# Router weights over 256 tokens: scattered with an adding DMA into a table in DRAM instead of built by one-hot products

## The chip, the cores and the metric

The kernel runs on one core of one Trainium2 chip. The metric is the device time of one execution in microseconds (us). TensorE (PE in the profile), VectorE (DVE), ScalarE (ACT) and GpSimd (POOL) compute, SyncE (SP) issues most DMAs; GpSimd issues the indexed ones.

## The reference

Two transformer blocks in a row on 512 tokens of width 1024: the first with gated delta rule and sparse attention, the second with two recurrent mixers and, last, a layer that picks 128 of 16384 small experts for each token. The change is in that last layer, which computes:

```python
s_top, i_top = lax.top_k(s, 16)                       # per head (8) and half (2), 128 keys each
cand = s_top[:, :, 0, :, None] + s_top[:, :, 1, None, :]
cand_idx = i_top[:, :, 0, :, None] * 128 + i_top[:, :, 1, None, :]
best, pos = lax.top_k(cand.reshape(n, 8, 256), 16)
idx = jnp.take_along_axis(cand_idx.reshape(n, 8, -1), pos, axis=-1)
w = jax.nn.softmax(best, axis=-1)
act = jax.nn.gelu(jnp.einsum('nhkd,nd->nhk', jnp.take(u_tab, idx, axis=0), hb))
out = jnp.einsum('nhk,nhkd->nd', w * act, jnp.take(v_tab, idx, axis=0))
```

## The kernel before, in words

The last layer is computed densely for 448 of the 512 tokens: for all 16384 experts the kernel takes the gelu of u times h, multiplies it by a table of weights W[expert, token] that is zero where the token did not choose the expert, and multiplies by v. The other 64 tokens gather their rows of u and v from DRAM by index.

*The u stage* (`u_pe`, `u_sc`, `u_ve`, `u_sy`) goes over 128 tiles of 128 experts. TensorE multiplies each fp32 product as three products of a high and a low half (`hh`, `hl` by `wh`, `wl`), 24 matmuls of 448 columns for a tile. ScalarE makes the high half `wh` of a weight pair, VectorE the low half `wl`, once for two tiles. ScalarE writes the gelu to `gst`, one of two buffers, and SP spills it to `gelu_spill`.

*The choice* runs woven into the u stage by a generator, `together(..., CHOOSE)`: CHOOSE steps of `choose` for each step of u. `top(j)` finds the experts of 128 tokens (j is 0 to 3) on VectorE and ends with the weights in `sel[:, 2]` (semaphore `wsel`). `hot(j)` builds the table for them, in quads of four tokens: VectorE makes one-hot matrices `Bh` and weighted one-hots `Ah`, TensorE multiplies them into 128 x 128 tables, ScalarE copies these to `stage`, SP spills 64 tokens at a time to `weight_spill`. 112 quads cover the 448 tokens.

*The v stage* goes over 64 pairs of tiles. `fetch` on SP brings back gelus and weights (`gv`, `wv`), `weigh` on VectorE multiplies them, `upper` and `lower` split the product in two halves `ph` and `pl`, and TensorE multiplies by v. The first three fetches, and the first `weigh` and `lower`, stand in the queues of SP and VectorE before the last tiles of the u stage (`start` at the end of `choose`). They wait until the whole table is in DRAM. All that stands behind them in the same queue waits too: on SP the loads of u and the gelu spills, on VectorE the low halves of u.

GpSimd does next to nothing before the v stage: one small DMA, then 128 gathers of 128 rows each (`gather_po`).

Of the kernel before, what the change touches and what calls it, by code (L numbers as in the profile page):

```python
# [22 lines left out]
class Line:  # L23
# [17 lines left out]
    def settle(self):  # L41
# [30 lines left out]
    [("g2_ex", 1), ("g3_ex", 1), ("sga", 16)],  # L72
    [("ve", 1356), ("fin", 8)],
# [97 lines left out]
ND = 512 - GT  # L171
# [100 lines left out]
def _build(nc, D, ctx):  # L272
# [90 lines left out]
    with ExitStack() as ar:  # L363
        x1 = sb("x1", [128, 8, 512], F32, ar)
        nb[1] = norm_bufs(1, ar)
        nb[2] = nb[1]
        ffh = sb("ffh", [128, 11, 512], R32, ar)
        ffl = sb("ffl", [128, 11, 512], R32, ar)
        fcv = [sb(f"fcv{j}", [128, 512], F32, ar) for j in range(6)]

    with ExitStack() as ar:
# [78 lines left out]
    with ExitStack() as ar:  # L450
        s_ = sb("s_", [128, 16, 128], F32, ar)
        sr = sb("sr", [128, 256], F32, ar)
        top = sb("top", [128, 16, 16], F32, ar)
        tix = sb("tix", [128, 16, 16], U32, ar)
        best = sb("best", [128, 8, 16], F32, ar)
        pix = sb("pix", [128, 8, 16], U32, ar)
        pa = sb("pa", [128, 8, 16], U32, ar)
        paf = sb("paf", [128, 2, 128], F32, ar)
        sel = sb("sel", [128, 3, 128], F32, ar)
        ijw = sb("ijw", [128, 3, 128], F32, ar)  # L460
        red8 = sb("red8", [128, 2, 8], F32, ar)
        tops = [top, cols[:, 0:256].rearrange("p (n k) -> p n k", n=16), top, top]
        tixs = [tix, cst[:, 256:512].bitcast(U32).rearrange("p (n k) -> p n k", n=16), tix, tix]
        Ah = [sb(f"Ah{j}", [128, 4, 128], F32, ar) for j in range(3)]
        Bh = [sb(f"Bh{j}", [128, 4, 128], F32, ar) for j in range(3)]
        stage = [sb(f"stage{j}", [128, 128, 64], F32, ar) for j in range(2)]
        gst = [sb(f"gst{j}", [128, ND], F32, ar) for j in range(2)]
    cand = eq = s_[:, :, :].rearrange("p (h x) k -> p h (x k)", h=8)

    with ExitStack() as ar:  # L470
        gv = [sb(f"gv{j}", [128, 2, ND], F32, ar) for j in range(3)]
        wv = [sb(f"wv{j}", [128, 7, 2, 64], F32, ar) for j in range(3)]
# [12 lines left out]
        nb[4] = norm_bufs(4, ar)  # L485
# [1225 lines left out]
    def ffn_ve(v):  # L1711
# [10 lines left out]
        for half in range(2):  # L1722
# [19 lines left out]
            for n in range(8):  # L1742
# [1149 lines left out]
    def top_ve(v, j):  # L2892
# [11 lines left out]
        v.settle()  # L2904
        for h in range(8):
            v.then_inc(tt(cand[:, h, :].rearrange("p (a b) -> p a b", a=16), bc(top[:, 2 * h, :], 16),
                          rep(top[:, 2 * h + 1, :], 16), A_), s("ve"))
        v.settle()
# [11 lines left out]
        for c in range(2):  # L2920
            v.settle()
            for h in range(8):
                e3 = eq[:, h, :].rearrange("p (k a) -> p k a", k=16)
                v.then_inc(tt(e3, bc(paf[:, c, 16 * h:16 * h + 16], 16), rep(C["iota"][:, 0:16], 16), ALU.is_equal),
                           s("ve"))
            yield
            v.settle()
            for h in range(8):
                e3 = eq[:, h, :].rearrange("p (k a) -> p k a", k=16)
                v.then_inc(tt(e3, e3, rep(top[:, 2 * h + c, :], 16), M), s("ve"))  # L2930
            yield
            if j and c == 0:
                v.wait_ge(s("ijw_mm"), j)
            v.settle()
# [9 lines left out]
        v.settle()  # L2944
        v.then_inc(tt(w3, w3, bc(red8[:, 1, :], 16), M), s("wsel"))
        if j == 0:
# [12 lines left out]


    def quads(j):

        return [(32 * j + q - 16, q) for q in range(16 if j == 0 else 0, 32)]

    WST = 256, 192

    def hot_pe(p, j):
# [3 lines left out]
        if j:  # L2971
            p.wait_ge(s("ijw"), j)
        for c in range(3):
# [5 lines left out]
        for t, q in quads(j):  # L2979
# [3 lines left out]
            for z in range(4):  # L2983
                ins = mm(p, bank[5 + t % 3][:, 128 * z:128 * z + 128], [(Ah[t % 3][:, z, :], Bh[t % 3][:, z, :])],
                         start=z == 0, check=False)
# [20 lines left out]
    def hot_ve(v, j):  # L3006
        for _ in range(3):
            yield
        v.wait_ge(s("ijw_mm"), j + 1)
        if j:  # L3010
            v.wait_ge(s("ab"), 32 * j - 16)
        v.then_inc(v.e.tensor_copy(flat(ijw[:, :, :]), bank[4][:, 0:384]), s("ijw"))
        v.settle()
        for t, q in quads(j):
            if t >= 3:
                v.wait_ge(s("ab_mm"), t - 2)
            v.e.tensor_tensor(Bh[t % 3][:, :, :], rep(C["iota"], 4), bc(ijw[:, 1, 4 * q:4 * q + 4], 128), ALU.is_equal)
            for z in range(4):
                k = 4 * q + z
                ins = v.e.tensor_scalar(Ah[t % 3][:, z, :], C["iota"], ijw[:, 0, k:k + 1], ijw[:, 2, k:k + 1],  # L3020
                                        ALU.is_equal, M)
            v.then_inc(ins, s("ab"))
            yield
        for _ in range(3):
            yield
# [76 lines left out]

    CHOOSE = 1.06

# [7 lines left out]
    def experts_ve(v):  # L3112
        arrive(v, 9)
        next_low(v, "u", 0)
        together((u_ve(v), 1), (choose_ve(v), CHOOSE))

# [18 lines left out]

    def weigh(v, i):
        v.wait_ge(s(f"gv{i % 3}"), 32 * (i // 3 + 1))
        g4 = gv[i % 3][:, :, :].rearrange("p x (b t) -> p x b t", b=7)
        for x in range(2):
            ins = v.e.tensor_tensor(g4[:, x], g4[:, x], wv[i % 3][:, :, x, :], M)  # L3140
        v.then_inc(ins, s("gw"))

# [74 lines left out]
    def start_pe(p):  # L3217
        p.wait_ge(s("ijw"), 4)
        turned_pe(p, 0)
# [30 lines left out]
    def v_pe(p):  # L3250
        p.wait_ge(s("stg"), 112)
        p.wait_ge(s("hT"), 2)
# [205 lines left out]
    def pool(e):  # L3458
        g = Line(e)
        gprep_po(g)  # L3460
        gather_po(g)

# [119 lines left out]
```

## Time and profile before

| | |
|---|---|
| median of 3 runs | 3344.34 us (3343.17 to 3346.76) |
| profiled execution, its own time | 3348.95 us |
| its span from first to last instruction | 3347.1 us |
| TensorE busy | 3244.8 us, 97% of the span |
| VectorE, ScalarE, GpSimd busy | 2110.6, 1188.1, 177.3 us |
| mean granted TensorE clock | 0.975 of 2.4 GHz |

A busy engine is one whose queue has an instruction under way. Times in rows are microseconds from the start of the span. The u stage lies at about 1975 to 2708 us, the v stage from there to 3327 us.

### The profile page before, as it was taken

Reading aid. Unit: us, or ns where it says so; the run is one execution under the profiler, and the core shown is the slowest. Engines: PE = TensorE matmul, PEld = TensorE weight load, DVE = VectorE, ACT = ScalarE, POOL = GpSimd, SP = SyncE. Lnnn points to the kernel's source line nnn. Section 1 sums busy time; section 2 is a strip of 40 time slices with the busy share of each in tenths; the row PEclk is TensorE's granted clock in tenths of the full one; section 3 lists DMA queues with packets and bytes.
Section 4 is the critical chain, followed back from the end, with each engine's and each line's share of the span. In section 5 each row is a group of like instructions: output and inputs, shape, how many; then the busy total and the mean of one; then the engine's idle time right before and its main releaser. Section 6 shows DMA issues by size and latency. Waiting matters only on the chain.

```text
span 3347.1 us, 43205 instructions
## 1 busy us (share of the span) xinstructions
PE 3244.8 (97%) x17902; PEld 2899.0 (87%) x17902; DVE 2110.6 (63%) x3746; ACT 1188.1 (35%) x1585; POOL 177.3 (5%) x137
## 2 busy tenths in 40 slices
PE   7998999999999999999999999999999999999998
PEld 7887887878789889888778788999999999999998
DVE  6446865747534434667544589796977356767775
ACT  2244233222223423555532223444445332222222
POOL 0000000000000000000000000000000013233230
PEclk9888999999999998999999999999999999999999
DMA  5232113232231242112233333545456678898884
GB/s 229 96 113 114 52 39 113 79 116 81 101 115 60 76 161 84 64 64 89 87 121 145 115 129 130 205 165 205 150 183 224 211 250 316 322 319 316 321 313 155
DMA packets 213763, 520.82 MB, mean 156 GB/s; under 512 B 12320, under 2 KB 143904, under 8 KB 178112
## 3 DMA queue, kind: packets, MB, share of 16 engines
q1 hardware_dynamic: 192944, 442.92, 36.8%
q0 software_dynamic: 18464, 67.15, 6.0%
q10 hardware_dynamic: 2160, 7.99, 0.6%
q8 instruction: 142, 2.33, 0.3%
q14 instruction: 53, 0.43, 0.0%
HBM read 437.23 MB, written 80.74 MB: 155 GB/s over the span
## 4 chain that ended last, share of the span: by engine, by line
PE 86%; DVE 7%; ACT 4%; issue 1%; DMA 1%; SPq 0%; DVEq 0%; ACTq 0%
PE bank L570 79%; PE bank L1233 2%; PE bank L634 1%; DVE wl L525 1%; PE bank L2504 1%; ACT wh L518 1%; PE bank L582 1%; PE bank L641 1%; ACT sgm L2572 1%; PE bank L1498 0%; PE bank L2513 0%; DVE ub L3186 0%; DMA cst<-in_consts 0%; DVE acc L148 0%; ACT sgm L2576 0%
## 5 line engine op out<-in xcount | busy, mean ns | idle before, releaser
L570 PE MATMUL bank<-hh,wh 128*128 128x512 f32 (+2 forms) x2512 | 949.5, 378 | 15.0 <-DVE hl L148 5.4
L570 PE MATMUL bank<-hl,wh 128*128 128x512 f32 (+2 forms) x2512 | 921.0, 367 | 0.0
L570 PE MATMUL bank<-hh,wl 128*128 128x512 f32 (+2 forms) x2512 | 920.0, 366 | 0.0
L525 DVE TENSOR_TENSOR wl<-ring,wh 128x2048 fp32r<-128x2048 f32 (+2 forms) x249 | 554.5, 2227 | 554.0 <-ACT wh L518 553.3
L518 ACT ACTIVATE wh<-ring 128x2048 fp32r<-128x2048 f32 (+2 forms) x249 | 463.4, 1861 | 879.2 <-PE bank L570 870.7
L570 PEld LDWEIGHTS bank<-hh,wh 128*128 128x128 f32 x2512 | 481.8, 192 | 83.7 <-issue 18.4
L570 PEld LDWEIGHTS bank<-hl,wh 128*128 128x128 f32 x2512 | 481.2, 192 | 64.1 <-issue 6.3
L570 PEld LDWEIGHTS bank<-hh,wl 128*128 128x128 f32 x2512 | 480.2, 191 | 61.8
L570 PE MATMUL bank<-ph,wh 128*128 128x448 f32 x1024 | 372.4, 364 | 5.3 <-DVE pl L3151 5.3
L570 PE MATMUL bank<-ph,wl 128*128 128x448 f32 x1024 | 370.7, 362 | 0.0
L570 PE MATMUL bank<-pl,wh 128*128 128x448 f32 x1024 | 369.9, 361 | 0.0
L570 PEld LDWEIGHTS bank<-ph,wh 128*128 128x128 f32 x1024 | 192.1, 188 | 19.9 <-issue 8.1
L570 PEld LDWEIGHTS bank<-ph,wl 128*128 128x128 f32 x1024 | 192.0, 188 | 13.6
L570 PEld LDWEIGHTS bank<-pl,wh 128*128 128x128 f32 x1024 | 191.9, 187 | 12.8
L3001 ACT ACTIVATE stage<-bank 128x512 f32<-128x512 f32 x112 | 123.7, 1108 | 94.7 <-PE bank L570 94.7
L570 PE MATMUL bank<-wh,hh 128*128 128x256 f32 (+2 forms) x520 | 156.2, 300 | 0.0
L570 PE MATMUL bank<-wl,hh 128*128 128x256 f32 (+2 forms) x520 | 151.1, 291 | 0.0
L570 PE MATMUL bank<-wh,hl 128*128 128x256 f32 (+2 forms) x520 | 151.0, 290 | 0.0
L3174 POOL DMA_INDIRECT ub<-in_urow,gsel x64 | 84.3, 1318 | 858.7 <-DMA weight_spill<-stage 537.1
L3020 DVE TENSOR_SCALAR Ah<-cst,ijw 128x128 f32<-128x128 f32 x448 | 124.5, 342 | 0.0
L570 PEld LDWEIGHTS bank<-Bh,Ah 128*128 128x128 f32 x896 | 116.9, 191 | 3.2 <-issue 0.4
L570 PE MATMUL bank<-Bh,Ah 128*128 128x128 f32 x896 | 117.7, 275 | 0.0
(516 smaller groups left out, 4348.6 us busy)
## 6 DMA issues: line engine op xcount, KB each, us to landing
ring<-in_v SPq DMA_DIRECT2D x68, 1024.0 KB
ring<-in_u SPq DMA_DIRECT2D x64, 1024.0 KB
gelu_spill<-gst SPq DMA_DIRECT2D x128, 224.0 KB, 1.9
weight_spill<-stage SPq DMA_DIRECT2D x28, 1024.0 KB, 8.6
gv<-gelu_spill SPq DMA_DIRECT2D x64, 448.0 KB, 4.6
wv<-weight_spill SPq DMA_DIRECT2D x64, 448.0 KB, 7.3
ring<-in_ada SPq DMA_DIRECT2D x24, 1024.0 KB
ring<-in_wup SPq DMA_DIRECT2D x22, 1024.0 KB
```

The costliest lines, as they stand in the source:

```text
L518: a.then_inc(a.e.activation(wh[q % 2][:, 0:n], ring[k % 4][:, 0:n], ACT.Copy), s("whi"))
L525: v.then_inc(v.e.tensor_tensor(wl[q % 2][:, 0:n], ring[k % 4][:, 0:n], wh[q % 2][:, 0:n].bitcast(F32), S_), s("parts"))
L570: ins = p.e.matmul(out, l, r, start=start and i == 0, stop=stop and i == len(pairs) - 1, skip_group_check=not check)
L582: return p.e.transpose(out, in_, ident[0:k, 0:k])
L634: ins = p.e.matmul(out[:, j:j + 1], sq[:, 128 * j:128 * j + 128], C["ones"][:, 0:1], start=start and j == 0, stop=stop, skip_group_check=True)
L641: ins = p.e.matmul(out[:, 128 * j:128 * j + 128], r[:, j:j + 1].to_broadcast([128, 128]), ident, start=j == 0, stop=True, skip_group_check ...
L1233: ins = p.e.matmul(ps[:, 128 * h:128 * h + 128], l, r, start=h == 0 and n_ == 0, stop=True, skip_group_check=True)
L2504: p.then_inc(p.e.matmul(bank[7][:, :], l, r, start=True, stop=True), s("ss_mm"))
L2572: ins = a.e.activation(sg[:, h, :], bank[3 + h // 4][:, 128 * (h % 4):128 * (h % 4) + 128], ACT.Abs, bias=nac[:, j, 8 * g + h:8 * g + h + 1])
L3001: a.then_inc(a.e.activation(place[:, :, 4 * (q % 16):4 * (q % 16) + 4].rearrange("p j t -> p t j"), quad(bank[5 + t % 3][:, :]), ACT.Copy) ...
L3020: ins = v.e.tensor_scalar(Ah[t % 3][:, z, :], C["iota"], ijw[:, 0, k:k + 1], ijw[:, 2, k:k + 1], ALU.is_equal, M)
L3174: g.e.indirect_dma_start(ub[n % 4][:, :], None, D["urow" if n < 64 else "vrow"], bass.IndirectOffsetOnAxis(gsel[:, 0, n % 64:n % 64 + 1], ...
```

## The change

The table for the 256 tokens of j = 1 and j = 2 is no longer built by `hot`. It is a second table in DRAM, `weight_scatter` (64 pairs x 2 x 128 x 256 values, 16.8 MB).

- It is cleared by 16 DMAs of 1 MB from a zeroed tile, issued from GpSimd during the first block's feed-forward part (`cleared_po`).
- VectorE computes for each chosen expert the flat place in the table (`sidx`) and leaves the weights in `swt`, one buffer for each of the two j (`top_ve`).
- GpSimd issues 2 x 128 indexed DMAs (`scatter_po`). Each writes 128 single values, one for each partition (token), to 128 places, adding to what is there. One DMA holds one of the 16 choices of one head. The 16 of a head follow each other freely; before the next head GpSimd waits until all earlier ones have landed, since two heads of one token may name the same expert.
- `hot` stays for j = 0 (16 quads) and j = 3 (32 quads), with two `Ah`/`Bh` buffers instead of three. 64 quads are gone.
- The first fetches wait for all 256 scatters (`scat`), a fetch is five DMAs instead of two, a `weigh` one instruction instead of two.
- In `top_ve` eight instructions on 256 elements become one on 2048, at five places. CHOOSE goes from 1.06 to 0.8.

```diff
+    SCATTER, HOT = (1, 2), (0, 3)
     def quads(j):
-        return [(32 * j + q - 16, q) for q in range(16 if j == 0 else 0, 32)]
+        return [(q - 16, q) for q in range(16, 32)] if j == 0 else [(16 + q, q) for q in range(32)]
...
+    def cleared_po(g):
+        arrive(g, 3)
+        g.then_inc(g.e.memset(zeros[:, :], 0.0), s("zr"))
+        g.wait_ge(s("zr"), 1)
+        flat_w = sw_.rearrange("i x b t -> (i x b t)").rearrange("(p n f) -> p n f", p=128, f=2048)
+        for n in range(16):
+            g.e.dma_start(flat_w[:, n, :], zeros[:, :]).then_inc(s("zw").sem, 16)
+
+    def scatter_po(g):
+        cells = sw_.rearrange("i x b t -> (i x b t)").unsqueeze(1)
+        g.wait_ge(s("zw"), 256)
+        for x, j in enumerate(SCATTER):
+            g.wait_ge(s("wsel"), j + 1)
+            g.wait_ge(s("scr"), x + 1)
+            for h in range(8):
+                if h:
+                    g.wait_ge(s("scat"), 16 * (128 * x + 16 * h))
+                for k in range(16 * h, 16 * h + 16):
+                    g.e.indirect_dma_start(cells, bass.IndirectOffsetOnAxis(sidx[x][:, k:k + 1], 0), swt[x][:, k:k + 1],
+                                           None, compute_op=ALU.add).then_inc(s("scat").sem, 16)
...
-        for j in range(3):
-            yield from weave((hot(j), 1), (top(j + 1), 0.75))
+        yield from weave((hot(0), 1), (top(1), 0.75))
+        yield from top(2)
+        yield from top(3)
         yield from hot(3)
         yield from start
...
-    CHOOSE = 1.06
+    CHOOSE = 0.8
...
         if i < 3:
-            y.wait_ge(s("ab_mm"), 112)
+            y.wait_ge(s("ab_mm"), 48)
+            y.wait_ge(s("scat"), 4096)
...
-        y.e.dma_start(wv[i % 3][:, :, :, :].rearrange("p b x t -> p b (x t)"),
-                      wd_[:, i].rearrange("b i x t -> i b (x t)")).then_inc(s(f"gv{i % 3}").sem, 16)
+        w = wv[i % 3]
+        y.e.dma_start(w[:, :, 64:320], sw_[i].rearrange("x b t -> b x t")).then_inc(s(f"gv{i % 3}").sem, 16)
+        for b, c in enumerate((0, 320, 384)):
+            y.e.dma_start(w[:, :, c:c + 64], wd_[b, i]).then_inc(s(f"gv{i % 3}").sem, 16)
...
     def pool(e):
         g = Line(e)
+        cleared_po(g)
         gprep_po(g)
+        scatter_po(g)
         gather_po(g)
```

GpSimd's queue from the second block on, before the change (`kdm` belongs to the recurrent mixer, `ub` are the gathers):

```order
L1957 TENSOR_TENSOR kdm<-kdm,km 128x16 [waits u_sr] x4
L3168 DMA gsel<-gsel 64x2x64 [waits gsel]
L3174 DMA ub<-in_urow,gsel 128x1024 [waits wst1,gcr]
L3174 DMA ub<-in_urow,gsel 128x1024 x3
L3174 DMA ub<-in_urow,gsel 128x1024 [waits gd] x60
```

The same stretch after the change; the pair of rows in its middle, 1 and 15 scatters, stands there 16 times in all:

```order
L1965 TENSOR_TENSOR kdm<-kdm,km 128x16 [waits u_sr] x4
L3008 DMA weight_scatter<-swt,sidx 4194304x1 [waits scr,h,zw]
L3008 DMA weight_scatter<-swt,sidx 4194304x1 x15
L3008 DMA weight_scatter<-swt,sidx 4194304x1 [waits scat]
...
L3214 DMA gsel<-gsel 64x2x64 [waits gsel]
L3220 DMA ub<-in_urow,gsel 128x1024 [waits wst1,gcr]
```

All 256 scatters stand ahead of GpSimd's first gather.

SP's queue at the first two fetches before the change, behind the 111th spill of a gelu tile (`in_u` are the loads of u):

```order
L3036 DMA weight_spill<-stage 128x16x128 [waits cvs]
L3036 DMA weight_spill<-stage 128x16x128 x3
L3100 DMA gelu_spill<-gst 128x448 [waits hi]
L3132 DMA gv<-gelu_spill 128x896 [waits gst1,wst0,wst1,gst0,cmp_h]
L3133 DMA wv<-weight_spill 128x7x128
L3132 DMA gv<-gelu_spill 128x896 [waits gst1,gst0]
L3133 DMA wv<-weight_spill 128x7x128
```

The same place after the change, now behind the 99th spill:

```order
L3145 DMA gelu_spill<-gst 128x448 [waits hi]
L3080 DMA weight_spill<-stage 128x16x128 [waits cvs]
L3080 DMA weight_spill<-stage 128x16x128 x3
L3179 DMA gv<-gelu_spill 128x896 [waits wst0,gst1,gst0,wst1,scat,cmp_h]
L3181 DMA wv<-weight_scatter 128x2x256
L3183 DMA wv<-weight_spill 128x2x64 x3
L3179 DMA gv<-gelu_spill 128x896 [waits gst1,gst0]
L3181 DMA wv<-weight_scatter 128x2x256
L3183 DMA wv<-weight_spill 128x2x64 x3
```

The fetch has moved 12 tiles of u forward, and waits for `scat` as well. On VectorE the end of `top(1)`, where the first scatters' weights come out, stands four low halves `wl` (eight tiles) later than before, and that of `top(2)` nine low halves behind it.

## Rows read from the trace of the kernel before

**Rows 1.** The page: busy shares, and the last chain by engine and line.

```profile
PE 3244.8 (97%) x17902; PEld 2899.0 (87%) x17902; DVE 2110.6 (63%) x3746; ACT 1188.1 (35%) x1585; POOL 177.3 (5%) x137
PE 86%; DVE 7%; ACT 4%; issue 1%; DMA 1%; SPq 0%; DVEq 0%; ACTq 0%
```

**Rows 2.** Stretches: length, busy time (count) by engine, clock, DMA share, GB/s.

```profile
540.00:640.00 100.00, 95.38 (x408) 77.17 (x407) 71.05 (x85) 29.41 (x33) 0.00 (x0) 0.95 0.23 81
...
2150.00:2250.00 100.00, 100.00 (x561) 94.01 (x560) 91.61 (x288) 43.06 (x43) 0.00 (x0) 1.00 0.46 159
...
2615.00:2650.00 35.00, 33.18 (x203) 29.81 (x202) 8.81 (x8) 7.93 (x10) 0.00 (x0) 0.97 0.98 296
...
2712.00:3327.00 615.00, 609.69 (x3054) 569.18 (x3053) 426.00 (x448) 172.18 (x130) 171.20 (x124) 1.00 0.85 303
```

**Rows 3.** TensorE's groups in 2150:2250.

```profile
L570 PE MATMUL bank<-hh,wh 128*128 128x448 f32 x139 | 52.1, 375 | 0.0
L570 PE MATMUL bank<-Bh,Ah 128*128 128x128 f32 x144 | 19.0, 275 | 0.0
```

**Rows 4.** The chain behind the table's last spill: start, length, what.

```profile
2614.10 1.02 ACT stage L3001
...
2625.64 8.93 DMA weight_spill<-stage
...
2634.69 0.33 SPq L3132
...
2636.15 7.07 DMA wv<-weight_spill
...
2645.40 2.22 DVE wl L525
...
2647.66 12.36 PE bank L570 x52
```

**Rows 5.** VectorE's timeline: the end of `top(1)`.

```profile
2142.72 0.29 DVE L2945 TENSOR_TENSOR sel<-sel,red 128x128 f32<-128x128 f32 x1
```

**Rows 6.** GpSimd's timeline: start, length, then in brackets its idle time before.

```profile
2043.09 0.81 POOL L3168 DMA_DIRECT2D gsel<-gsel  x1 [904.67 <-DVE gsel L2949]
2581.05 1.01 POOL L3174 DMA_INDIRECT ub<-in_urow,gsel  x1 [537.14 <-DMA weight_spill<-stage]
2582.36 0.95 POOL L3174 DMA_INDIRECT ub<-in_urow,gsel  x1 [0.30 <-issue]
2583.62 0.94 POOL L3174 DMA_INDIRECT ub<-in_urow,gsel  x1 [0.30 <-issue]
...
2996.88 1.85 POOL L3174 DMA_INDIRECT ub<-in_vrow,gsel  x1 [0.31 <-issue]
...
3014.79 1.93 POOL L3174 DMA_INDIRECT ub<-in_vrow,gsel  x1 [7.38 <-DVE acc L148]
3017.03 0.94 POOL L3174 DMA_INDIRECT ub<-in_vrow,gsel  x1 [0.30 <-issue]
```

**Rows 7.** VectorE's timeline beside those gathers.

```profile
2582.42 1.11 DVE L3020 TENSOR_SCALAR Ah<-cst,ijw 128x128 f32<-128x128 f32 x4
...
2996.84 1.09 DVE L3151 TENSOR_TENSOR pl<-gv,ph 128x896 fp32r<-128x896 f32 x1
...
3013.24 2.67 DVE L148 SCALAR_TENSOR_TENSOR acc<-ub,gwt,acc 128x1024 f32<-128x1024 f32 x2
```

**Rows 8.** VectorE's groups over the u stage, 1975:2712.

```profile
L525 DVE TENSOR_TENSOR wl<-ring,wh 128x2048 fp32r<-128x2048 f32 x64 | 146.4, 2288 | 145.1 <-ACT wh L518 144.8
L3020 DVE TENSOR_SCALAR Ah<-cst,ijw 128x128 f32<-128x128 f32 x448 | 124.5, 342 | 0.0
L3017 DVE TENSOR_TENSOR Bh<-cst,ijw 128x512 f32<-128x512 f32 x112 | 76.4, 682 | 11.5 <-PE bank L570 11.3
```

**Rows 9.** Landing time of the tile `gsel`, the one plain DMA from GpSimd.

```profile
DMA to landing us min/median/max: 2.6/2.6/2.6
```

**Rows 10.** DMA issues: count, size, median us to landing.

```profile
gelu_spill<-gst SPq DMA_DIRECT2D x128, 224.0 KB, 1.9
weight_spill<-stage SPq DMA_DIRECT2D x28, 1024.0 KB, 8.6
```

**Rows 11.** What SP's queue waited for in 1975:3340: us, times, longest.

```profile
SPq L3132 <- DVE pl L3151: 489.1, 60, 9.5
```

More of the change, by code:

```diff
@@ L463, in _build @@
         tixs = [tix, cst[:, 256:512].bitcast(U32).rearrange("p (n k) -> p n k", n=16), tix, tix]
-        Ah = [sb(f"Ah{j}", [128, 4, 128], F32, ar) for j in range(3)]
-        Bh = [sb(f"Bh{j}", [128, 4, 128], F32, ar) for j in range(3)]
+        Ah = [sb(f"Ah{j}", [128, 4, 128], F32, ar) for j in range(2)]
+        Bh = [sb(f"Bh{j}", [128, 4, 128], F32, ar) for j in range(2)]
+        sidx = [sb(f"sidx{j}", [128, 128], U32, ar) for j in range(2)]
+        swt = [sb(f"swt{j}", [128, 128], F32, ar) for j in range(2)]
+        sdiag = sb("sdiag", [128, 128], F32, ar)
+        stok = sb("stok", [128, 16], F32, ar)
+        sb("past_scatter", [128, 368], F32, ar)
         stage = [sb(f"stage{j}", [128, 128, 64], F32, ar) for j in range(2)]
@@ L471, in _build @@
         gv = [sb(f"gv{j}", [128, 2, ND], F32, ar) for j in range(3)]
-        wv = [sb(f"wv{j}", [128, 7, 2, 64], F32, ar) for j in range(3)]
+        wv = [sb(f"wv{j}", [128, 2, ND], F32, ar) for j in range(3)]
         sb("past_choice", [128, 1936], F32, ar)
@@ L2904, in top_ve @@
         v.settle()
-        for h in range(8):
-            v.then_inc(tt(cand[:, h, :].rearrange("p (a b) -> p a b", a=16), bc(top[:, 2 * h, :], 16),
-                          rep(top[:, 2 * h + 1, :], 16), A_), s("ve"))
+        pairs = top[:, :, :].rearrange("p (h c) k -> p h c k", c=2)
+        v.then_inc(tt(cand[:, :, :].rearrange("p h (a b) -> p h a b", a=16),
+                      pairs[:, :, 0, :].unsqueeze(3).to_broadcast([128, 8, 16, 16]),
+                      pairs[:, :, 1, :].unsqueeze(2).to_broadcast([128, 8, 16, 16]), A_), s("ve"))
         v.settle()
@@ L2921, in top_ve @@
             v.settle()
[L2922 to L2925, printed above, removed]
+            places = eq[:, :, :].rearrange("p h (k a) -> p (h k) a", a=16)
+            v.then_inc(tt(places, bc(paf[:, c, :], 16), rep(C["iota"][:, 0:16], 128), ALU.is_equal), s("ve"))
             yield
             v.settle()
-            for h in range(8):
-                e3 = eq[:, h, :].rearrange("p (k a) -> p k a", k=16)
-                v.then_inc(tt(e3, e3, rep(top[:, 2 * h + c, :], 16), M), s("ve"))
+            e4 = eq[:, :, :].rearrange("p h (k a) -> p h k a", k=16)
+            v.then_inc(tt(e4, e4, pairs[:, :, c, :].unsqueeze(2).to_broadcast([128, 8, 16, 16]), M), s("ve"))
             yield
-            if j and c == 0:
-                v.wait_ge(s("ijw_mm"), j)
+            if j == 1 and c == 0:
+                v.wait_ge(s("ijw_mm"), 1)
             v.settle()
@@ L2944, in top_ve @@
         v.settle()
-        v.then_inc(tt(w3, w3, bc(red8[:, 1, :], 16), M), s("wsel"))
+        if j in SCATTER:
+            x = SCATTER.index(j)
+            v.then_inc(tt(swt[x][:, :].rearrange("p (h k) -> p h k", h=8), w3, bc(red8[:, 1, :], 16), M), s("wsel"))
+            v.then_inc(stt(v.e, sel[:, 0, :], sel[:, 1, :], 128.0, sel[:, 0, :], M, A_), s("ve"))
+            v.settle()
+            v.then_inc(ts(v.e, sidx[x][:, :], sel[:, 0, :], 256.0, M, stok[:, x:x + 1], A_), s("scr"))
+        else:
+            v.then_inc(tt(w3, w3, bc(red8[:, 1, :], 16), M), s("wsel"))
         if j == 0:
@@ L3008, in hot_ve @@
             yield
-        v.wait_ge(s("ijw_mm"), j + 1)
+        v.wait_ge(s("ijw_mm"), HOT.index(j) + 1)
         if j:
-            v.wait_ge(s("ab"), 32 * j - 16)
+            v.wait_ge(s("ab"), 16)
         v.then_inc(v.e.tensor_copy(flat(ijw[:, :, :]), bank[4][:, 0:384]), s("ijw"))
@@ L3014, in hot_ve @@
         for t, q in quads(j):
[L3015 to L3017 removed]
+            if t >= 2:
+                v.wait_ge(s("ab_mm"), t - 1)
+            v.e.tensor_tensor(Bh[t % 2][:, :, :], rep(C["iota"], 4), bc(ijw[:, 1, 4 * q:4 * q + 4], 128), ALU.is_equal)
             for z in range(4):
                 k = 4 * q + z
[L3020 removed]
+                ins = v.e.tensor_scalar(Ah[t % 2][:, z, :], C["iota"], ijw[:, 0, k:k + 1], ijw[:, 2, k:k + 1],
                                         ALU.is_equal, M)
@@ L3132, in fetch @@
         y.e.dma_start(gv[i % 3][:, :, :], gd_[i]).then_inc(s(f"gv{i % 3}").sem, 16)
-        y.e.dma_start(wv[i % 3][:, :, :, :].rearrange("p b x t -> p b (x t)"),
-                      wd_[:, i].rearrange("b i x t -> i b (x t)")).then_inc(s(f"gv{i % 3}").sem, 16)
+        w = wv[i % 3]
+        y.e.dma_start(w[:, :, 64:320], sw_[i].rearrange("x b t -> b x t")).then_inc(s(f"gv{i % 3}").sem, 16)
+        for b, c in enumerate((0, 320, 384)):
+            y.e.dma_start(w[:, :, c:c + 64], wd_[b, i]).then_inc(s(f"gv{i % 3}").sem, 16)
     def weigh(v, i):
[L3137 to L3141, printed above, removed]
+        v.wait_ge(s(f"gv{i % 3}"), 80 * (i // 3 + 1))
+        v.then_inc(v.e.tensor_tensor(gv[i % 3][:, :, :], gv[i % 3][:, :, :], wv[i % 3][:, :, :], M), s("gw"))
     def upper(a, i):
```

35 lines of the change are left out of this document (23 added, 12 removed).

## The prediction, on record before the run

> **What bounds the kernel now.** I read the busy shares first, then the stretches of the last layer, then the chain behind the table's last spill. TensorE is busy for 97% of the span and holds 86% of the chain that ended last [rows 1]. Inside the u stage it is busy for 100.00 of 100.00 us while VectorE is too at 91.61 [rows 2]: VectorE is nearly full there, but TensorE waits for nothing. So an instruction taken off TensorE there is time saved, if nothing else becomes late.
>
> The one tight place is where the table is finished. The last `stage` copy is at 2614.1; its spill lands at 2634.6; only then does SP issue the first fetch (2634.69), whose data land at 2643.2; VectorE, which has been standing in `weigh`, then makes the low half that is due, and TensorE starts on it at 2647.66 [rows 4]. TensorE lost 1.8 us of 35 there [rows 2]. The reader should see two things. The chain from the table's completion to TensorE is 13 us long, and TensorE has no reserve behind it: whatever makes the fetch later than "last `stage` copy plus 20.5 us" stops TensorE for as long.
>
> **What the change takes away.** 64 quads, each 4 one-hot products, each of 2 records: 512 of the `Bh,Ah` matmuls. In 2150:2250 TensorE ran 3 x 139 matmuls of 448 columns and 144 of these [rows 3]. One of 448 columns costs 0.2005 us: the v stage runs 64 x 48 = 3072 of them in 615 us [rows 2]. So 417 x 0.2005 = 83.6 us, and the other 16.4 us are 144 records: 0.114 us each. 512 x 0.114 = 58 us. **Term 1: -58 us.** The copies to `stage`, 16 of the 28 MB of spills, and 64 x (0.68 + 4 x 0.28) = 115 us of VectorE go too (0.28 is a quarter of the 1.11 us of four [rows 7]); they were hidden under TensorE and give nothing by themselves. The merged instructions in `top_ve` are hidden in the same way.
>
> **What it adds.** *Clearing.* 16 MB of stores during the first feed-forward part, where the DMA engines are at 0.23 and the load is 81 GB/s [rows 2]. At the v stage's 303 GB/s they take 55 us beside the loads, which run several tiles ahead: 0, and at most a few us if a weight comes late. *Fetch.* Five DMAs instead of two. In the v stage SP waits 489 us for VectorE's `pl` [rows 11], so 64 x 3 issues of about 0.43 us are covered: 0. For the first fetches nothing covers them: 2 x 3 x 0.43, **term 2: +3 us**.
>
> *The scatters.* They start when `top(1)` ends: 2143.0 before [rows 5], now 8 tiles later. A tile is 24 x 0.2005 = 4.81 us, so 2143 + 38.5 = 2182. `top(2)` ends 18 tiles, 87 us, behind that, sooner than 128 scatters can be issued, so GpSimd runs through. The fetch would be ready at 2634.6 less 12 tiles (57.7) less the 58 us of missing quads: 2519. GpSimd has 337 us for 256 scatters: 1.32 us for each, everything included, and 1.53 with term 1 spent.
>
> No row shows a scatter with single values or with an addition. The nearest is a gather of GpSimd: also 128 indexed rows in one DMA. Back to back it takes 0.94 us, with 0.30 us between two [rows 6], a period of 1.25: 256 x 1.25 = 320 us. Lower bound of one: the plain DMA from GpSimd, 0.81 + 0.30 = 1.11, 284 us. Upper bound: if an adding transfer must describe two reads where a copy describes one, the 0.94 doubles: 2.19, 561 us. I take 1.25, since count of rows and index are the same.
>
> *Restarts.* 15 times GpSimd waits for the last scatter to land. The plain DMA from GpSimd landed after 2.6 us [rows 9], a gelu spill after 1.9, a weight spill after 8.6 [rows 10]. With a landing after 4 us, between these, and 1.25 already counted, 15 x 2.75 = 41 us; with 2.6 us it is 20, with 8.6 it is 110.
>
> *VectorE holds GpSimd up.* A gather is not always 0.94 us. The one at 2996.88 started 0.04 us after `pl`, a TENSOR_TENSOR with both inputs in SBUF that ran 2996.84 to 2997.93, and ended at 2998.73, that is 0.80 us after it. The one at 3014.79 started inside two SCALAR_TENSOR_TENSOR that ended at 3015.91, and ended 0.81 us after them. The gather at 2582.36 lay beside four TENSOR_SCALAR and took its 0.95 [rows 6, 7]. So an instruction with two SBUF tensors makes a gather wait until it is over. In the v stage there were two or three gathers for each pair of tiles; now there is one each 1.25 us, so every `wl` of 2.29 us [rows 8] catches one. It waits for what is left, on average 2.29 - 1.25/2 = 1.67 us. 337 us hold 337/9.63 = 35 `wl`: 58 us. The merged instructions of 2048 elements have two SBUF inputs too, five in each of `top(2)` and `top(3)`, about 2.2 us each if they run at `wl`'s rate: 10 x 1.6 = 16 us. The 32 `Bh` of `hot(3)`, 0.68 us: 0.68/1.25 of them hit, for 0.34 us, 6 us. Together 80 us, bounds 0 and about 110 (each `Ah` held too).
>
> The Trainium skill, "SBUF — State Buffer", section "Who interferes with whom", says the same of VectorE instructions with two SBUF inputs beside a GpSimd instruction that reads SBUF, but also that a `tensor_tensor` was not seen to hold up descriptor generation. The row at 2996.88 shows one that did. By that last rule the sum would be the first rival below.
>
> 320 + 41 + 80 = 441 us, so the last scatter lands at 2182 + 441 = 2623, 104 us after the fetch could have gone. SP stands in the first fetch all that time. Behind it are the gelu spills: with two `gst` buffers ScalarE stops two tiles later, and with it `wh`; VectorE stops in `weigh`, and with it `wl`. TensorE follows at once, since rows 4's chain left it nothing. **Term 3: +104 us.** GpSimd's gathers begin behind the scatters but before the v stage, so nothing is late next.
>
> The sum is -58 + 3 + 104 = +49 us. The profiled execution took 3348.95, 4.6 above the median, and its span plus 1.85; the difference applies to both: 3344.3 + 49 = 3393 us at the median.
>
> **The rivals.**
> *The scatters fit (other side: faster).* If `wl` does not hold scatters up, because their index is read in a moment that mostly falls elsewhere, they take 361 us and end at 2543, 24 us late: -58 + 3 + 24 = -31, 3313 us. With the short restarts (20) they are 3 us late: 3292 us. For it speaks the gather beside four TENSOR_SCALAR, against it both long gathers of rows 6. It decides when a scatter costs less than 1.53 us with everything: from there down the kernel is faster. Chance 0.32.
> *The addition costs more.* 32768 single values are each read, added and written. If that costs the 0.94 again, 240 us more: 3393 + 240 = 3633 us; half of it, 3513. For it: an add reads two things; against: no row has one. Chance 0.24. The Trainium skill, "Collectives: The Full Stack", section "The bandwidth ceiling: the fold count and why AG ≠ RS ≠ AR", says that a reducing transfer passes two read descriptors for each piece where a copy passes one, and ran at about half the rate. No row here shows it; by it this rival would hold in full.
> *It balances.* Between the two, gain and wait are equal, at 1.53 us for a scatter: 3344 us. Chance 0.04.
>
> **How the numbers follow.** The forecast, scatters at a gather's price with VectorE in the way, has 0.40; its own range is 3355 to 3450, from 40 us less blocking to 8.6 us landings. A measurement tells 0.2% (7 us) from no change. Faster: 0.32. Same: 0.04. Slower: 0.40 + 0.24 = 0.64. The range goes from 3294, which leaves out only scatters fully hidden (0.06), to 3560, between the half and the full price of the addition (0.12 above it).
>
> **What would show it.** Term 1: in the u stage 24 matmuls a tile and no gap of their own, the last `stage` copy near 2498. Term 3: GpSimd's scatters from about 2182 to about 2623, most of 0.94 us, some near 2.5 that end 0.8 us behind a `wl`; SP waiting for a scatter for about 100 us; TensorE idle for as long around 2530 to 2630. Term 2: the first `weigh` some 11 us after the last landing. I am wrong if GpSimd is done before 2519 (faster by the full 58), if scatters back to back take much more than 0.94 with VectorE idle, which shows in the last ones, when VectorE stands still, or if the DMA engines and not GpSimd set the pace, seen in waits for `scat` much longer than 3 us.

## The result, and the profile after

| | before | after |
|---|---|---|
| median | 3344.34 us (5 runs, 3338.11 to 3350.36) | 3512.65 us (5 runs, 3511.1 to 3518.81) |
| profiled execution, span | 3347.1 us | 3509.3 us |
| mean granted TensorE clock | 0.975 | 0.947 |

The change costs 168 us: 1.0509 times the time before (95% interval 1.0496 to 1.0521). The forecast was 3393 us, +49, in a range of 3294 to 3560. Direction, place and chain were as forecast; the size was not.

The page of after: span, busy shares, the granted clock in 40 slices, the packets of GpSimd's DMAs, the last chain by engine, and two of the costliest groups.

```profile
span 3509.3 us, 41968 instructions
PE 3185.0 (91%) x17384; PEld 2838.7 (81%) x17384; DVE 1994.0 (57%) x3227; ACT 1119.3 (32%) x1521; POOL 628.2 (18%) x410
...
PEclk9889999999999989999999999999955799999999
...
q0 software_dynamic: 57632, 84.08, 9.5%
...
PE 72%; POOL 12%; DVE 6%; issue 4%; ACT 4%; DMA 2%; SPq 0%; DVEq 0%; ACTq 0%; POOLq 0%
...
L577 PE MATMUL bank<-hh,wh 128*128 128x512 f32 (+2 forms) x2512 | 945.3, 376 | 237.2 <-ACT gst L3128 213.9
...
L3008 POOL DMA_INDIRECT weight_scatter<-swt,sidx x256 | 440.9, 1722 | 1160.0 <-DVE sidx L144 1046.6
```

Beside [rows 1], TensorE is busy for 59.8 us less (3244.8 to 3185.0, 518 recorded matmuls fewer): the 58 us of the missing quads are there. GpSimd now holds 12% of the chain, and TensorE has one idle time of 213.9 us. The average of 91% says little: all of it is in one place.

Four stretches of after (length, busy time and count of PE, PEld, DVE, ACT, POOL, clock, DMA share, GB/s): the scatters beside the u stage, the stop, the clearing, the v stage.

```profile
2181.00:2515.00 334.00, 320.96 (x1708) 296.75 (x1707) 245.48 (x613) 125.52 (x127) 265.46 (x144) 0.99 0.62 164
2540.00:2680.00 140.00, 1.87 (x10) 1.39 (x8) 0.00 (x0) 0.00 (x0) 109.01 (x71) 0.52 0.20 0
540.00:640.00 100.00, 95.21 (x414) 77.08 (x414) 72.43 (x86) 30.24 (x36) 0.00 (x0) 0.97 0.46 180
2862.00:3477.00 615.00, 610.25 (x3048) 569.63 (x3046) 424.21 (x385) 176.03 (x134) 170.77 (x124) 1.00 0.88 306
```

The last two answer to [rows 2] (95.38 and 609.69 us of TensorE there): clearing the table is free although the DMA share doubles to 0.46, and a fetch of five DMAs costs the v stage nothing. In 2540:2680 only GpSimd works.

The scatters as a group (duration min/median/max in ns, first and last start), and what GpSimd's idle time before them ended with (us, times).

```profile
L3008 POOL DMA_INDIRECT weight_scatter<-swt,sidx x256: 1548/1550/3879, 2182.8 to 2735.5; - x128
...
  issue: 84.0, 241
  DMA weight_scatter<-swt,sidx: 29.3, 14
```

A scatter takes 1.55 us, and as the minimum is 1.548, never less. The 0.94 us of a gather [rows 6] was the forecast. The last lands at 2738.4, not 2623. The group of the 100 scatters that start in 2542:2738, when VectorE stands still, has the same mean, so it is not VectorE that makes them long:

```profile
L3008 POOL DMA_INDIRECT weight_scatter<-swt,sidx x100 | 155.1, 1551 | 41.5 <-issue 31.5 <-DMA weight_scatter<-swt,sidx 10.0
```

The waits of after: what the engines, and in the last row SP's queue, waited for in 1975:2900 (us, times, longest).

```profile
ACT gst L3128 <- DMA gelu_spill<-gst: 234.9, 5, 225.9
DVE gv L3187 <- DMA wv<-weight_spill: 219.5, 2, 214.7
PE bank L577 <- ACT gst L3128: 213.9, 1, 213.9
...
PE bank L577 <- DVE wl L532: 13.0, 9, 2.5
...
SPq L33 <- DMA weight_scatter<-swt,sidx: 212.9, 1, 212.9
```

SP stands 212.9 us in front of the first fetch, with all inputs but the scatters there; ScalarE, VectorE and TensorE stand behind it, each by about as much. TensorE stops 16 us after SP does (it works until 2541.9) and starts again 17 us after SP, so its stop is as long as the fetch is late. The critical chain of after at the end of the stop (start, length, what):

```profile
2735.49 2.91 DMA weight_scatter<-swt,sidx
2738.40 0.02 SPq L33
...
2750.55 4.65 DMA gelu_spill<-gst
...
2755.22 0.55 ACT gst L3128
...
2755.82 4.48 PE bank L577 x11
```

From the last scatter's landing (2738.40) to TensorE's start it is 17.4 us, 12 of them SP's issue of three fetches (15 DMAs) ahead of the gelu spill for which ScalarE waits. It was 13 us behind the last `weight_spill` [rows 4], and there `weigh` released TensorE, here the gelu spill. The stop has a small cost behind it as well: the first 14 matmuls follow each other at 0.37 us, with the granted clock at 0.54 in 2755:2762, and the next ones at 0.20 with 1.00, which is 2.4 us.

### The profile page after: what moved, and what is told of

It is laid out like the page before. It is cut to its first block, busy times and chain, and to the rows that moved or that the text cites. A ratio compares the mean times of both kernels' runs of the same rounds, so it can differ in the third digit from the quotient of the medians.

```text
span 3509.3 us, 41968 instructions
## 1 busy us (share of the span) xinstructions
PE 3185.0 (91%) x17384; PEld 2838.7 (81%) x17384; DVE 1994.0 (57%) x3227; ACT 1119.3 (32%) x1521; POOL 628.2 (18%) x410
## 4 chain that ended last, share of the span: by engine, by line
PE 72%; POOL 12%; DVE 6%; issue 4%; ACT 4%; DMA 2%; SPq 0%; DVEq 0%; ACTq 0%; POOLq 0%
PE bank L577 66%; POOL weight_scatter L3008 12%; PE bank L1240 2%; DMA weight_scatter<-swt,sidx 2%; PE bank L641 1%; PE bank L2512 1%; ACT wh L525 1%; DVE wl L532 1%; PE bank L648 1%; ACT sgm L2580 1%; PE bank L589 1%; PE bank L1505 0%; DMA cst<-in_consts 0%; PE bank L2521 0%; DVE ub L3232 0%
## 5 line engine op out<-in xcount | busy, mean ns | idle before, releaser
L577 PE MATMUL bank<-hh,wh 128*128 128x512 f32 (+2 forms) x2512 | 945.3, 376 | 237.2 <-ACT gst L3128 213.9
L525 ACT ACTIVATE wh<-ring 128x2048 fp32r<-128x2048 f32 (+2 forms) x249 | 463.3, 1861 | 930.4 <-PE bank L577 922.0
L3008 POOL DMA_INDIRECT weight_scatter<-swt,sidx x256 | 440.9, 1722 | 1160.0 <-DVE sidx L144 1046.6
L3187 DVE TENSOR_TENSOR gv<-gv,wv 128x896 f32<-128x896 f32 x64 | 69.4, 1084 | 219.5 <-DMA wv<-weight_spill 219.5
L3128 ACT ACTIVATE gst<-bank 128x448 f32<-128x448 f32 x128 | 68.3, 534 | 371.9 <-DMA gelu_spill<-gst 234.9
L3220 POOL DMA_INDIRECT ub<-in_vrow,gsel x64 | 90.2, 1410 | 202.0 <-DVE acc L148 179.6
```

The source lines that it names most:

```text
L525: a.then_inc(a.e.activation(wh[q % 2][:, 0:n], ring[k % 4][:, 0:n], ACT.Copy), s("whi"))
L577: ins = p.e.matmul(out, l, r, start=start and i == 0, stop=stop and i == len(pairs) - 1, skip_group_check=not check)
L3008: g.e.indirect_dma_start(cells, bass.IndirectOffsetOnAxis(sidx[x][:, k:k + 1], 0), swt[x][:, k:k + 1], None, compute_op=ALU.add).then_inc( ...
L3128: a.then_inc(a.e.activation(gst[t % 2][:, :], bank[t % 4][:, 0:ND], ACT.Gelu_apprx_tanh), s("ge_u"))
L3187: v.then_inc(v.e.tensor_tensor(gv[i % 3][:, :, :], gv[i % 3][:, :, :], wv[i % 3][:, :, :], M), s("gw"))
L3220: g.e.indirect_dma_start(ub[n % 4][:, :], None, D["urow" if n < 64 else "vrow"], bass.IndirectOffsetOnAxis(gsel[:, 0, n % 64:n % 64 + 1], ...
```

## The experiments

Times are medians, and a ratio is to runs of the kernel before that stand beside them. The edits show the lines that matter; sizes, buffer counts and semaphore numbers that follow from them are left out. Two theories were put against each other first: the addition makes a scatter long (A), or the 128 single values or indices do (B); and whether the scatters are the only loss.

**1. Scatters without the addition** (two heads that name one expert for a token then overwrite each other: the sums are left out).

```diff
 g.e.indirect_dma_start(cells, bass.IndirectOffsetOnAxis(sidx[x][:, k:k + 1], 0), swt[x][:, k:k + 1],
-                       None, compute_op=ALU.add).then_inc(s("scat").sem, 16)
+                       None).then_inc(s("scat").sem, 16)
```

> The 256 scatters write without adding (where two heads of a token name the same expert, the last one stays: this leaves out the addition). Theory A, the addition makes a scatter dearer than a gather: back to back it falls from 1.55 to about 0.94 us, the scatters take some 156 us less, TensorE's stop of 214 us falls to about 60, time about 3357 us. Theory B, single values written to DRAM cost it and not the addition: 1.55 us stays and the time stays within 5 us of 3513.

3379.47 us, ratio 1.009 [1.007, 1.011]. Its page has the packets of GpSimd's DMAs:

```profile
q0 software_dynamic: 28960, 84.08, 7.4%
```

The group of its scatters (ns min/median/max):

```profile
L3008 POOL DMA_INDIRECT weight_scatter<-swt,sidx x256: 962/967/3532, 2184.6 to 2605.4; - x128
```

Its waits, TensorE's and SP's:

```profile
PE bank L577 <- ACT gst L3128: 48.3, 1, 48.3
...
PE bank L577 <- issue: 19.1, 22, 2.5
...
SPq L33 <- DMA weight_scatter<-swt,sidx: 74.8, 1, 74.8
```

Theory A: 0.967 us, a gather's price within 0.03, in place of 1.550. The addition costs 0.58 us for each DMA, and without it the median goes from 3512.65 to 3379.47, 133 us less. It shows in the packets too: 28672 fewer, 112 for each of the 256 DMAs. The run took about 20 us more than expected; TensorE stood 19.1 us with nothing in the profile that it waited for ("issue"), of which more under 6. The executions were 3372.48, 3377.91, 3381.03 and 3463.31 us; the last, at a mean granted clock of 0.949, isn't in the ratio and has no trace, so whether it had more of these waits is open.

**2. Only j = 1 scattered** (the weights of 128 tokens are left out).

```diff
-        for x, j in enumerate(SCATTER):
+        for x, j in enumerate(SCATTER[:1]):
...
-            y.wait_ge(s("scat"), 4096)
+            y.wait_ge(s("scat"), 2048)
```

> Only the scatters of j = 1 are issued and waited for; the weights of 128 tokens are left out of the table. Theory: the wait for the scatters is the whole loss, and all other parts of the change (clearing, five DMAs for a fetch, merged instructions, CHOOSE 0.8) cost nothing: the last scatter lands near 2182 + 278 = 2460, before the fetch can go at 2519, TensorE does not stop, and the time is 3344 - 58 + 3 = 3289 us. Rival: one of the other parts costs something too: then the time is above 3300 us by as much.

3300.87 us, ratio 0.9864 [0.9848, 0.9881]. The 128 scatters, 1.55 us each, lie between 2189.3 and 2480.0, before the fetch is ready. SP waits for none; TensorE waits for this:

```profile
PE bank L577 <- DVE wl L532: 14.2, 10, 2.5
```

So term 1 is real, and the loss is the scatters' length. The rival of the expectation has a small part in it: 43 us came, not 58. 9.3 of the missing 15 are a wait for `wl` that before doesn't have, which in after lies ahead of the stop and costs nothing there; most of the rest is that the traced execution of before lay 4.6 us above its median (the two spans differ by 46.8). That the wait comes since `top(2)` and `top(3)`, without quads between them, run too densely at CHOOSE 0.8, and VectorE makes a low half late, is what 5 tests.

**3. Scatters of 64 values** (half of the scattered weights are left out).

```diff
-  bass.IndirectOffsetOnAxis(sidx[x][:, k:k + 1], 0), swt[x][:, k:k + 1],
+  bass.IndirectOffsetOnAxis(sidx[x][0:64, k:k + 1], 0), swt[x][0:64, k:k + 1],
```

> Each of the 256 scatters has 64 rows instead of 128 (the weights of the other 64 tokens of each j are left out). If the price goes by the row, 1.55 falls to about 0.8 us, the scatters take some 190 us less and end near 2548, time about 3300 us. If it is mostly fixed for each DMA, 1.55 stays and the time stays within 15 us of 3513.

3480.74 us, ratio 1.0405 [1.0388, 1.0422]; TensorE stops for 181.2 us. That is 32 us under the 3513 of a fixed price and 181 above the 3300 of a price by the row. From its page GpSimd's packets, then the group of its scatters:

```profile
q0 software_dynamic: 41248, 84.01, 8.8%
```

```profile
L3008 POOL DMA_INDIRECT weight_scatter<-swt,sidx x256: 1389/1397/4147, 2184.0 to 2703.2; - x128
```

Half of the values take 0.15 us off 1.55: nine tenths of the price stay with the DMA. The packets, though, go with the values (64 fewer for 64 fewer values), so the packets are not what the time goes by.

**4. CHOOSE 0.65**: the steps of VectorE's second queue are spread over more tiles; nothing is left out.

```diff
-    CHOOSE = 0.8
+    CHOOSE = 0.65
```

> CHOOSE 0.65 instead of 0.8, nothing left out: the scatters start about 9 tiles (43 us) later, and the first fetch moves from tile 99 to about tile 122. Theory: the scatters keep their 556 us and end near 2781, but nearly all of the u stage is done by then, so the v stage can start some 20 us after that, near 2800 instead of 2862: time about 3450 us, still slower than 3344. Rival: if the scatters were slowed by the work beside them and not by their own price, they end earlier and the time falls further, towards 3400.

3456.39 us, ratio 1.0328 [1.0311, 1.0346]. The scatters run from 2225.8 to 2786.3, 8 us longer than in after, but the table's other half is finished later too, and u tiles are made meanwhile. SP waits 162.4 us, TensorE 3.1 for `wl`, and the stop has moved to the v stage:

```profile
PE bank L577 <- DVE pl L3197: 173.9, 2, 173.6
```

**5. Both, 2 and 4** (the weights of 128 tokens are left out).

```diff
-        for x, j in enumerate(SCATTER):
+        for x, j in enumerate(SCATTER[:1]):
...
-            y.wait_ge(s("scat"), 4096)
+            y.wait_ge(s("scat"), 2048)
...
-    CHOOSE = 0.8
+    CHOOSE = 0.65
```

> As the run with the scatters of j = 1 alone (the weights of 128 tokens are left out), with CHOOSE 0.65. That run was 43 us faster than before instead of 58; TensorE waited 13 us for low halves wl in 2185:2370, where top(2) and top(3) run without a hot beside them. Theory: VectorE had more work there for each pair of tiles than TensorE; spread thinner the wait falls to about 3 us, time about 3291 us. Rival: the 13 us come from GpSimd holding VectorE up at the shared port, or from something else that CHOOSE does not touch: then 3301 stays.

3294.58 us, ratio 0.9855 [0.984, 0.987]. The wait for `wl` falls from 14.2 to 3.5 us, beside the same 128 scatters, so it isn't they that make `wl` late; waits for `pl` of 7.2 us come (6.2 in one). That is 6 us by the medians, but the intervals of the ratios overlap: the wait for `wl` moved as the theory says, but its worth is not measured.

**6. 64 values and no addition** (leaves out what 1 and 3 do).

```diff
-  bass.IndirectOffsetOnAxis(sidx[x][:, k:k + 1], 0), swt[x][:, k:k + 1],
-  None, compute_op=ALU.add)
+  bass.IndirectOffsetOnAxis(sidx[x][0:64, k:k + 1], 0), swt[x][0:64, k:k + 1],
+  None)
```

> 64 rows in each scatter and no addition (half of the weights left out). The adding scatter cost 1.55 us with 128 rows and 1.39 with 64, the plain one 0.97 with 128. If the addition is a fixed price for each DMA, the plain one with 64 rows costs 0.97 - 0.16 = 0.81; if part of it goes by the row, more, up to 0.97. Time about 3345 us, since the scatters end some 30 us earlier than in the run without the addition (3379).

3582.81 us, ratio 1.0715 [1.0698, 1.0731]: a clear miss, the slowest of all, with the shortest scatters. Their group, then TensorE's wait:

```profile
L3008 POOL DMA_INDIRECT weight_scatter<-swt,sidx x256: 886/892/2760, 2183.6 to 2579.9; - x128
```

```profile
PE bank L577 <- issue: 246.4, 137, 3.7
```

The stretches 2250:2350 and 2350:2450 of this kernel (busy PE, PEld, DVE, ACT, POOL, clock, DMA share, GB/s), and two rows of TensorE's timeline:

```profile
2250.00:2350.00 100.00, 19.16 (x36) 10.26 (x36) 13.38 (x46) 2.34 (x2) 71.43 (x79) 0.50 0.05 13
2350.00:2450.00 100.00, 80.83 (x351) 69.25 (x351) 62.12 (x151) 23.77 (x25) 24.25 (x26) 0.84 0.35 119
```

```profile
2484.71 0.53 PE L577 MATMUL bank<-hh,wh 128*128 128x448 f32 x1 [1.57 <-issue]
2487.51 0.53 PE L577 MATMUL bank<-hl,wh 128*128 128x448 f32 x1 [2.27 <-issue]
```

For pricing it still serves: 0.89 against 1.39 us, so the addition costs 0.50 at 64 values and 0.58 at 128. But while the scatters run, TensorE starts a matmul only every 2.80 us, at half clock (1.2 GHz), VectorE has 46 instructions in 100 us, and the DMA engines are at 0.05. TensorE waits for no engine and no transfer that the profile shows; ScalarE and VectorE also have waits that it puts down to a queue it doesn't know (208 and 59 us). The second stretch shows that the scatters are the cause: GpSimd, whose first 128 were done, stands there for 67 us before the next 128, and in 2362:2422 TensorE has 275 matmuls in 60 us at clock 0.93. Some 10 us after the scatters begin again it is slow again, and after the last ones the usual rate is back. Experiment 1 shows the same rows for a short time around 2530 to 2560 (matmuls of 0.53 us at clock 0.58, behind waits for "issue" of up to 1.9 us). How plain single-value scatters hold TensorE up, and why 64 values are worse than 128, is open.

**7. Scatter only what fits.** If 128 scatters are hidden and 256 are not, j = 1 alone should be scattered and 0, 2 and 3 built as before: 32 quads off, 32 x 8 x 0.114 = 29 us to gain. Nothing is left out, here and in 8 to 10.

```diff
-    SCATTER, HOT = (1, 2), (0, 3)
+    SCATTER, HOT = (1,), (0, 2, 3)
...
         yield from top(2)
-        yield from top(3)
+        yield from weave((hot(2), 1), (top(3), 0.75))
         yield from hot(3)
...
-    CHOOSE = 0.8
+    CHOOSE = 0.9
```

> Nothing left out: only j = 1 is scattered (128 scatters, with the addition), hot stays for j = 0, 2 and 3 (80 quads), top(3) woven with hot(2) again, CHOOSE 0.9. Theory: the scatters run from about 2170 to 2450 and are done long before the fetch at about 2600, so the saving is that of 32 quads, 32 x 0.91 = 29 us: 3315 us, up to 3320 if VectorE is late in the unwoven top(2). Rival: the scatters or the many small DMAs of a fetch (seven) cost something of their own: 3330 and above.

3332.07 us, ratio 0.9967 [0.9955, 0.9979]. No wait for scatters, but 16.9 us for `wl` in four waits (three of them, 12.3 us, where `top(2)` runs with no quads between), 12.0 more than before has: most of the 18 us by which the gain falls short.

**8. Scatter j = 0 and j = 1**, which are chosen first, so that 256 scatters start 122 us earlier. `hot(0)` was half as long as the others, so this takes 48 quads off: 44 us.

```diff
-    SCATTER, HOT = (1, 2), (0, 3)
+    SCATTER, HOT = (0, 1), (2, 3)
...
-        yield from weave((hot(0), 1), (top(1), 0.75))
+        yield from top(1)
         yield from top(2)
-        yield from top(3)
+        yield from weave((hot(2), 1), (top(3), 0.75))
...
-    CHOOSE = 0.8
+    CHOOSE = 0.73
```

> Nothing left out: j = 0 and 1 are scattered (256 scatters, adding, 192 dense tokens), hot for j = 2 and 3 (64 quads), CHOOSE 0.73. The scatters start when top(0) ends, at about 2072 instead of 2182, and take 556 us, to about 2628; the fetch stands at tile 122 and can go at about 2620 to 2630. Theory (only the start and the length of the scatters against the fetch decide): TensorE stops for 10 us or less, 48 quads are saved (43 us), VectorE's lateness costs up to 10: 3305 to 3320 us. Rival: with the scatters this late something else of the v stage's start is late, the gathers behind them or the data of the first fetches: 3330 and above.

3339.13 us, ratio 0.9984 [0.9975, 0.9993]. The scatters run from 2060.6 to 2657.2, 44 us longer than in after: 47.9 us of restarts in place of 29.3 and 463.3 busy in place of 440.9, probably because all of them now lie beside a working VectorE. SP waits 36.1 us and TensorE 38.7, which is nearly the gain.

**9. 7 with `hot(0)` spread over `top(1)` and `top(2)`**, so that no `top` runs alone.

```diff
-        yield from weave((hot(0), 1), (top(1), 0.75))
-        yield from top(2)
+        yield from weave((hot(0), 0.5), (both(top(1), top(2)), 1))
         yield from weave((hot(2), 1), (top(3), 0.75))
...
-    CHOOSE = 0.9
+    CHOOSE = 0.82
```

> Nothing left out: as the run with j = 1 alone scattered and 80 quads, but the quads of hot(0) are spread over top(1) and top(2), CHOOSE 0.82. There TensorE waited 12.3 us for low halves in 2163:2300, where top(2) ran alone, and the gain was 11 us of the 29 that 32 quads are worth. Theory: VectorE's surplus in that stretch is the missing part; spread over two tops it goes, and the time is about 3318 us. Rival: the order does not matter and the rest of the loss has another place: 3328 to 3336 as before.

**3316.09 us, ratio 0.9914 [0.9901, 0.9928]**: the fastest kernel that computes everything, 28.4 us faster than before, of 29 that the missing quads are worth. Against 7 it changes two things, the weaving and CHOOSE (0.9 to 0.82), and they weren't separated: either can have taken the density away. Its scatters as a group, then TensorE's one wait for `wl` (before had 4.9 us of it in the u stage):

```profile
L3009 POOL DMA_INDIRECT weight_scatter<-swt,sidx x128: 1548/1551/3862, 2124.0 to 2427.0; - x128
```

```profile
PE bank L577 <- DVE wl L532: 5.5, 1, 5.5
```

**10. 8 with the first head plain.** The first head of each j writes into a cleared table, so needs no addition.

```diff
-  None, compute_op=ALU.add)
+  None, **(dict(compute_op=ALU.add) if h else {}))
```

> Nothing left out: as the run with j = 0 and 1 scattered, but the scatters of the first head of each j write without adding, which is the same in a cleared table. 32 of 256 scatters fall from 1.55 to 0.97 us. Theory: there TensorE stopped 38.7 us for the last scatters, so the 32 x 0.58 = 19 us come off the time in full: about 3321 us. Rival: only the adding ones' landings set the pace, or plain scatters hold TensorE's instructions up as with 64 plain rows: 3335 us or more.

3329.11 us, ratio 0.9957 [0.9943, 0.997], 10 us better than 8 by the medians. 26 of the 32 plain ones take 0.95 to 1.25 us, and the 32 together 14 us less than in 8, but the other 224 take 10 us more, so that in the profiled execution GpSimd is busy for 459.8 us (463.3 in 8), the last scatter starts at 2657.8 and SP waits 37.8 us, as in 8; that execution took 3341.34 us, the longest of its five. So the trace doesn't show what the medians gained, and this stays open.

**The books.** If the quads (0.91 us each) and TensorE's waits are all there is, their sum should be the measured difference. Waits are those that before has not (4.9 us for `wl` and 5.3 for `pl` taken off). They are read from the profiled executions, so the sum is held against the difference of these spans too (before: 3347.1); the last column is that of the medians.

| kernel | quads | stop or `pl` | `wl` | sum | spans | medians |
|---|---|---|---|---|---|---|
| after | -58 | +213.9 | +8.1 | +164 | +162.2 | +168.3 |
| 3, 64 values | -58 | +181.2 | +8.9 | +132 | +132.1 | +136.6 |
| 4, CHOOSE 0.65 | -58 | +173.0 | -1.8 | +113 | +110.3 | +112.3 |
| 2, half | -58 | 0 | +9.3 | -49 | -46.8 | -43.3 |
| 5, half, 0.65 | -58 | +5.7 | -1.4 | -54 | -53.5 | -48.4 |
| 7, one scattered | -29 | 0 | +12.0 | -17 | -19.8 | -10.9 |
| 8, first two | -44 | +38.7 | -4.3 | -9 | -9.8 | -3.9 |
| 9, one, woven | -29 | 0 | +0.6 | -28 | -33.6 | -28.4 |
| 10, 8 with plain | -44 | +39.9 | -4.2 | -8 | -7.6 | -15.4 |

By the spans all but 9 close within 3 us (9 is off by 6), by the medians within 8. 1 and 6 don't close by waits alone, since TensorE also ran at half clock: its busy time is 3208.4 and 3231.5 us against 3185.0 of after. With "issue" and that added the sums are +37 and +235, and the spans differ by 32.1 and 233.4.

## Why the prediction was wrong, point by point

- **Term 1, -58 us: right.** TensorE's busy time fell by 59.8 us; experiments 2 and 9 turn it into time.
- **Clearing, five DMAs a fetch, merged instructions at 0: right for this kernel.** The third holds only since the stop lies behind it: 13.0 us of waits for `wl` in 2185:2370 come with it, 2 and 7 show that they cost once the scatters fit, and 9 that they need not come. No run has the short instructions in the new order, so the part of the merged ones isn't separated. The prediction had called the merged instructions hidden, and had not asked how densely `top(2)` and `top(3)` follow each other when no quads lie between them.
- **Term 2, +3 us: right in kind.** Three fetches, not two, are issued ahead of the gelu spill, and the restart takes 17.4 us, where 13 and 3 were forecast.
- **Term 3, +104 us: the mechanism right, its size wrong; this is the step that failed.** "I take 1.25, since count of rows and index are the same." One scatter with its gap is 1.85, not 1.25 (1.55 for 0.94 without the gap): 256 x 0.61 = +156 us. The addition was put at nothing in this term, and experiment 1 shows that it is nearly all of the difference. The term's other parts were too high: restarts 29.3 us for 41 (there are 14 of them, not 15), VectorE's hold-ups 440.9 - 256 x 1.55 = 44 us for 80. The gaps are 84 us in 241, 0.35 each for 0.30. 556 us in place of 441, so the fetch goes 213 us late where 104 were forecast (from 2525.4, when the last `weight_spill` had landed; 2519 was forecast).
- **The start, 2182: right** (2182.8). The u stage's other points came within 8 us: the last `stage` copy began at 2506.18, not 2498, through the waits for `wl`.
- **VectorE holds GpSimd up: right, and weaker.** VectorE's rows and GpSimd's beside them in after:

```profile
2204.72 2.27 DVE L532 TENSOR_TENSOR wl<-ring,wh 128x2048 fp32r<-128x2048 f32 x1
...
2226.29 2.29 DVE L2914 TENSOR_TENSOR s_<-top 128x2048 f32<-128x2048 f32 x1
```

```profile
2203.32 1.55 POOL L3008 DMA_INDIRECT weight_scatter<-swt,sidx  x1 [0.30 <-issue]
2205.18 3.24 POOL L3008 DMA_INDIRECT weight_scatter<-swt,sidx  x1 [0.30 <-issue]
2208.72 1.55 POOL L3008 DMA_INDIRECT weight_scatter<-swt,sidx  x1 [0.30 <-issue]
...
2226.72 3.29 POOL L3008 DMA_INDIRECT weight_scatter<-swt,sidx  x1 [0.30 <-issue]
```

  A scatter that meets a TENSOR_TENSOR with two SBUF inputs ends 1.43 us behind it (2206.99 to 2208.42, 2228.58 to 2230.01). The Trainium skill, "SBUF — State Buffer", "Who interferes with whom", says that such an instruction contends with a GpSimd one that reads SBUF, but that a `tensor_tensor` was not seen to stall a DMA; these rows show two that did. The forecast of 80 us was too high because VectorE worked beside at most 156 of the 256 scatters (42 of those took over 1.7 us, 43 us too much together), and stood still beside the last 100.
- **The rival "the addition costs more" is what happened**, at 0.58 of the 0.94 it allowed for: between its half (3513 us) and its full price (3633). That the result stands on 3513 is partly luck, since +156 was met by -48 us in the other two parts. The Trainium skill, "Collectives: The Full Stack", "The bandwidth ceiling: the fold count and why AG ≠ RS ≠ AR", has a reducing transfer at about half a copy's rate, by two read descriptors for each piece. The trace agrees in the direction. An addition took a DMA from 32 packets to 144 (by the differences between after, 1, 2 and 3), 4.5 times, and its time on GpSimd from 0.97 to 1.55 us, 1.6 times, not 2. On the DMA engines it cost far more: in 2300:2350 GpSimd's queue took 15.2% of them for 23 adding scatters, and 1.4% for 31 plain ones. But they had room: GpSimd waited only 29.3 of 556 us for landings.
- **"The scatters fit"** named the point that decides, 1.53 us for one with everything. The measured 556 / 256 = 2.17 is far beyond it; even the plain ones of experiment 1, at 1.65 with everything (2184.6 to 2605.4, and the landing), are above it.

What could have been seen: the prediction priced an unknown operation by what it shares with a gather (rows, index) and left out what differs (the addition), though it held a rival for just that, and its bounds were 1.11 and 2.19. With the middle of the bounds, 1.65 for one, 102 us more and 3495 us would have come out.

## What to carry to other kernels

An operation with an unknown price, issued hundreds of times in a row, must be multiplied before it is chosen: here 0.58 us for an addition became 133 us of the time. Count what fits into the time until the result is needed, and move only that to the slower engine: half of the change (9) wins where the whole loses, since a queue that is done early costs nothing and one that is late stops every engine behind it. When work leaves one engine, look at what it had kept apart on the others: `top` alone made `wl` late, `top` woven with quads, or spread over more tiles, did not.

## What the runs showed of the hardware

- An indexed DMA from GpSimd of 128 single values takes 0.97 us to issue plain, 1.55 adding; with 64 values 0.89 and 1.39. To these come 0.30 us between two (after, 1, 3 and 6).
- The adding form makes one packet more for each value more, the plain one does not: 144 and 80 packets for 128 and 64 values adding, 32 plain.
- A run of plain single-value scatters can hold TensorE up without a wait that the profile shows: with 64 values it had a matmul only every 2.80 us and stood 246.4 us in all, with 128 values 19.1 us; in a pause of the scatters it ran as usual. TensorE had no such wait beside the adding ones. The cause is open.
